# Two of six feed-forwards read their rows from a view 32 bytes in front of the first

## What is computed

```python
def swiglu(x, w_gu, w_down):
    g, u = jnp.split(x @ w_gu, 2, axis=-1)
    return (jax.nn.silu(g) * u) @ w_down
...
    y = modulate(rmsnorm(h, norm_ffn2[l]), sh3, sc3)
    h = h + 0.5 * gt3[:, None, :] * swiglu(y, w_ffn2_gu[l], w_ffn2_down[l])
```

## Time and profile before

| | |
|---|---|
| Three timed runs | 2493.82, 2497.54 and 2498.13 us, median 2497.54 us |
| Profiled execution, span | 2492.1 us, 39,334 instructions |
| TensorE busy | 2410.8 us (97%), 14,736 matmuls |
| VectorE, ScalarE, GpSimd busy | 1511.0, 892.0, 382.4 us |
| Mean granted TensorE clock | 0.985 |

### The profile page before, as it was taken

How to read it: one execution, slowest core, us unless ns; L and a number is a source line. 1 busy time by engine, 2 the same in 40 slices (tenths; PEclk the granted TensorE clock), 3 DMA queues, 4 the chain that set the end, 5 groups by cost and what they waited for, 6 DMA issues and landing times.

```text
span 2492.1 us, 39334 instructions
## 1 busy us (share of the span) xinstructions
PE 2410.8 (97%) x14736; PEld 2129.9 (85%) x14736; DVE 1511.0 (61%) x2434; ACT 892.0 (36%) x1103; POOL 382.4 (15%) x353
## 2 busy tenths in 40 slices
PE   6998989999999998999999999999999999999999
PEld 4998879999888888867778888888888889999999
DVE  7676768967878665355477786652222274555544
ACT  4443455454222223332232222242222242344443
POOL 2110531211111102332311111001110000000110
PEclk6999999999999999999999999999999999999999
DMA  7877746854655554211135555522222242135455
GB/s 280 284 263 274 259 141 222 275 196 159 218 185 194 180 168 150 81 64 51 68 115 202 185 179 190 172 85 101 101 80 90 99 149 81 68 104 184 169 186 168
DMA packets 79879, 400.19 MB, mean 161 GB/s; under 512 B 8817, under 2 KB 12913, under 8 KB 54705
## 3 DMA queue, kind: packets, MB, share of 16 engines
q1 hardware_dynamic: 77216, 393.39, 45.6%
q0 software_dynamic: 1056, 3.67, 0.5%
q10 hardware_dynamic: 1520, 1.95, 0.2%
HBM read 396.88 MB, written 2.10 MB: 160 GB/s over the span
## 4 chain that ended last, share of the span: by engine, by line
PE 46%; DVE 3%; ACT 1%; issue 0%; DMA 0%; ACTq 0%; DVEq 0%; SPq 0%
PE pg L1181 14%; PE pg L1182 13%; PE pg L1183 13%; PE pg L1359 1%; PE pg L1358 1%; PE pg L1360 1%; PE px L2003 1%; DVE wlo L2075 1%; PE px L1989 1%; DVE TMP L2244 0%; ACT whi L686 0%; PE px L1977 0%; DVE wlo L2080 0%; DMA raw<-w_d 0%; DVE Yl L2235 0%
## 5 line engine op out<-in xcount | busy, mean ns | idle before, releaser
L2080 DVE TENSOR_TENSOR wlo<-raw,whi 128x2048 fp32r<-128x2048 f32 (+1 forms) x202 | 415.6, 2057 | 504.0 <-ACT whi L691 503.5
L691 ACT ACTIVATE whi<-raw 128x2048 fp32r<-128x2048 f32 (+1 forms) x202 | 348.7, 1726 | 537.4 <-PE pg L1183 470.5
L1181 PE MATMUL pg<-Yh,whi 128*128 128x512 f32 (+1 forms) x1352 | 518.1, 383 | 11.6 <-DVE Yl L2303 2.6
L1182 PE MATMUL pg<-Yl,whi 128*128 128x512 f32 (+1 forms) x1352 | 513.0, 379 | 0.0
L1183 PE MATMUL pg<-Yh,wlo 128*128 128x512 f32 (+1 forms) x1352 | 512.8, 379 | 0.0
L1181 PE MATMUL pg<-YhB,whi 128*128 128x256 f32 (+1 forms) x1504 | 435.3, 289 | 20.5 <-DVE YlB L2235 7.6
L1182 PE MATMUL pg<-YlB,whi 128*128 128x256 f32 (+1 forms) x1504 | 428.4, 285 | 0.0
L1183 PE MATMUL pg<-YhB,wlo 128*128 128x256 f32 (+1 forms) x1504 | 428.2, 285 | 0.0
L1181 PEld LDWEIGHTS pg<-YhB,whi 128*128 128x128 f32 x1504 | 286.8, 191 | 31.2 <-issue 18.1
L1181 PEld LDWEIGHTS pg<-Yh,whi 128*128 128x128 f32 x1352 | 256.1, 189 | 67.2 <-issue 8.7
L1183 PEld LDWEIGHTS pg<-Yh,wlo 128*128 128x128 f32 x1352 | 256.1, 189 | 47.8
(11 more groups left out here) (378 smaller groups left out, 3642.1 us busy)
## 6 DMA issues: line engine op xcount, KB each, us to landing
raw<-w_t SPq DMA_DIRECT2D x194, 1024.0 KB, 5.1
ada<-w_ada SPq DMA_DIRECT2D x200, 512.0 KB, 3.6
raw<-w_d SPq DMA_DIRECT2D x96, 704.0 KB, 4.2
ADA<-w_ada SPq DMA_DIRECT2D x16, 512.0 KB, 13.9
NB<-na_bias POOLq DMA_DIRECT2D x8, 256.0 KB, 3.0
X<-x_t ACTq DMA_DIRECT2D x2, 512.0 KB, 15.8
spectrum<-HF POOLq DMA_DIRECT2D x1, 1024.0 KB, 10.3
X<-ctx_t SPq DMA_DIRECT2D x1, 1024.0 KB, 7.3
```

The source lines that it names most:

```text
L691: act.activation(whi[:, n % 2, 0:size], raw[:, n % 2, 0:size], ACT.Copy).then_inc(sem["hi_ready"], 1)
L1181: pe.matmul(out, w_hi, y_hi, start=first, stop=False)
L1182: pe.matmul(out, w_hi, y_lo, start=False, stop=False)
L2080: dve.tensor_tensor(wlo[:, n % 2, 0:size], raw[:, n % 2, 0:size], whi[:, n % 2, 0:size].bitcast(F32), ALU.subtract)\
```

## The change

A third view is added, 32 bytes in front of the first and so half-way between the two. The second feed-forward of layer 0 (`l0_gu2`, `l0_down2`, 512 tokens, first view before) and the second of layer 1, the last one (`l1_gu2`, `l1_down2`, 256 tokens, second view before) use it: their norms (`l0_2`, `l1_2`) write the normalised rows into it, their inner rows go into it, and their matmuls read from it. In `lead_pair`, which read `Hh` and `Hl` by name, the view is now asked for; for the two other down phases that end in it the answer is the same as before. No instruction is added, removed or moved on any engine: the two programs have the same 10,535 instructions in the same order, and differ in addresses.

```diff
-SHORT_ROWS = ("b1_0", "b1_gu1", "b1_1", "b1_in", "merge", "b1_out", "b1_2", "b1_gu2", "l1_1", "l1_in", "l1_2", "l1_gu2")
+MIDDLE_ROWS = ("l0_2", "l0_gu2", "l1_2", "l1_gu2")
+SHORT_ROWS = ("b1_0", "b1_gu1", "b1_1", "b1_in", "merge", "b1_out", "b1_2", "b1_gu2", "l1_1", "l1_in")
...
+    YhC = nc.alloc_sbuf_tensor_at("YhC", [P, 4096], F32R, offset=y_at - 32)
+    YlC = nc.alloc_sbuf_tensor_at("YlC", [P, 4096], F32R, offset=yl_at - 32)
...
+    HhC = nc.alloc_sbuf_tensor_at("HhC", [P, KF, 512], F32R, offset=region - 32)
+    HlC = nc.alloc_sbuf_tensor_at("HlC", [P, KF, 512], F32R, offset=hl_at - 32)
...
     def row_view(name):
 
+        if name in MIDDLE_ROWS:
+            return YhC8, YlC8
         return (YhB8, YlB8) if name in SHORT_ROWS else (Yh8, Yl8)
 
     def inner_of(name):
 
+        if name in ("l0_gu2", "l0_down2", "l1_gu2", "l1_down2"):
+            return HhC, HlC
         return (HhB, HlB) if INFO[name][2] == 256 else (Hh, Hl)
...
-                    return three(pg[1][:, stream, cols], whi[:, half, w], wlo[:, half, w], Hh[:, 11 * half + kt, cols], Hl[:, 11 * half + kt, cols],
+                    return three(pg[1][:, stream, cols], whi[:, half, w], wlo[:, half, w], inner_of(down)[0][:, 11 * half + kt, cols], inner_of(down)[1][:, 11 * half + kt, cols],
```

More of the change, by code:

```diff
@@ L309, in rhs_r @@
         return t[:, :].rearrange("p (c n) -> p c n", n=256)
-    Yh8, Yl8, YhB8, YlB8 = rhs_t(Yh), rhs_t(Yl), rhs_t(YhB), rhs_t(YlB)
+    Yh8, Yl8, YhB8, YlB8, YhC8, YlC8 = rhs_t(Yh), rhs_t(Yl), rhs_t(YhB), rhs_t(YlB), rhs_t(YhC), rhs_t(YlC)
     def row_view(name):
+        if name in MIDDLE_ROWS:
+            return YhC8, YlC8
         return (YhB8, YlB8) if name in SHORT_ROWS else (Yh8, Yl8)
     def inner_of(name):
+        if name in ("l0_gu2", "l0_down2", "l1_gu2", "l1_down2"):
+            return HhC, HlC
         return (HhB, HlB) if INFO[name][2] == 256 else (Hh, Hl)
```

## The result

Over six timed runs of each kernel the changed kernel took 2510.7 us in the median (2505.6 to 2518.3) and the kernel before 2495.7 (2489.3 to 2502.8). The ratio is **1.0064, 95% interval 1.0050 to 1.0078**: slower by 0.64%, about 16 us. The profiled execution after has a span of 2508.7 us, 16.6 us more than that of before.

What follows compares the result with a forecast made beforehand. TensorE was taken to bound the kernel, busy 97% of the span. Terms +5.2 + 5.2 - 0.4 = +10.0 us on 2497.5 gave 2507.5 us; forecast's own range 2502.5 to 2512.5, whole range 2493 to 2521 us.

Steps and rivals of the forecast that it cites:

- Direction and bound: In the four changed phases TensorE alone sets the time, so longer matmuls go into it one to one; slower 0.59.
- The term for 512 columns: l0_gu2 and l0_down2, first view to third: 1518 matmuls times 3.4 ns, +5.2 us, between 0 and +10.3.
- equally near both rows, so I take the mean: Third view lies 32 bytes from either known view, so 512 columns were priced at 230.1 ns, between 226.7 and 233.5.
- The term for 256 columns: l1_gu2 and l1_down2, second view to third: 1584 matmuls times 3.3 ns, +5.2 us, between 0 and +10.3.
- one width keeps its good pitch and the other takes the bad one: Second way to the middle of the sum: only one of 512 and 256 columns loses, +10.3 us either way.
- both widths in the bad state: Rival: third view as bad as the bad view for 512 and 256 columns, +20.6 us, 2518 us; chance 18%.
- The sign that it named: Pitch on YhC and HhC between 227 and 233 ns in l0_gu2 and l0_down2 in the profile after.
- No change: Rival: all pitches in the four phases stay, sum -0.9 to 0 us, 2497 us; chance 24%.
- The floor falls: Rival: third view escapes a sixteenth lost at both widths, gaining 30.9 us, 2466.6 us; gain over 5 us has 17%.
- The two pitches of the second view: 256 columns at 113.2 or 118.0 ns; in l1_in worth 2.8 us of either sign, left out of the sum.

## Why the prediction held, and where its sum was too small

**Direction and bound: right, and shown.** TensorE alone set the time of the four phases; 16.2 us more in them made 16.6 us more span, with no new wait and no other engine late. The order of instructions, the tail (2.80 us) and the norms stayed. Groups after, the norms' writes on the third view:

```profile
L743 ACT ACTIVATE YhC<-TMP,MOD 128x256 fp32r<-128x256 f32 x24 | 11.1, 503 | 9.3 <-DVE TMP L2253 9.3
L2244 DVE SCALAR_TENSOR_TENSOR YlC<-TMP,MOD,YhC 128x256 fp32r<-128x256 f32 x24 | 10.8, 480 | 0.8 <-ACT YhC L743 0.8
```

503 and 480 ns are the 501 to 506 and 480 of the earlier trace rows: these writes took the same time in all three views.

**The term for 512 columns: mis-sized by half.** It was 1518 times 3.4 ns, +5.2 us; it measured 1518 times 6.66, **+10.1**, its upper bound. The step that failed is "equally near both rows, so I take the mean". Nearness is no measure here: 16 bytes off the good place cost what 64 do.

**The term for 256 columns: mis-sized by a third.** It was +5.2 us and came to 1056 times 4.9 plus 528 times 4.7 ns, **+7.7** (6.6 in the two windows, which leave out a block and from which the wait in l1_down2 went). Here the mean was wrong for another reason: 113.2 and 119.7 are no ends of one scale, but one special place and an ordinary level of 117 to 120. lead_pair gained 0.2 us where 0.4 was forecast.

The sum by pitches is +17.6 us for the forecast's +10.0; the six runs of each say 16 (12 to 20). The reading "one width keeps its good pitch and the other takes the bad one", offered as a second way to the same sum, is false, since both lost. The nearest of the rivals was **both widths in the bad state**: at 512 exactly so, at 256 three quarters of the way.

That the time came out 3.2 us from the forecast (2510.7 for 2507.5) is partly luck. The forecast started from the median of three runs, 2497.5 us; over six runs the kernel before has 2495.7, so the medians differ by 15.0 us where 10.0 was forecast. That lies on the seam between the two cases that the prediction kept apart, its forecast (+5 to +15) and both widths bad (+15 to +23), and the pitches are nearer to the second. The sign that it named, 227 to 233 ns with 512 columns, was passed by 0.3.

**The other rivals.** *No change* is refuted by the pitches: a start moved by 16 bytes alone costs 6.7 ns at 512 columns. By the Trainium skill (SBUF — State Buffer, DMA port swizzle, the note on cachelines) an access that crosses into a new 16-byte line pays a penalty. By that alone no place tried here would differ, since all are whole lines; the traces, with 226.7 against 233.3 ns, show that it is not all that counts in a matmul's reads. *The floor falls* is refuted for the places tried: over eight starts for the rows, in steps of 16 bytes, and weights at three, no steady stretch at the full clock lay below 226.7 or 113.3 ns. The estimate from the Trainium skill (TensorE: Matmul & The Clock Gate, Back-to-back issue gap), 215.8 and 109.2 ns, showed in no run; the section calls its formula that of a matmul by itself. The two pitches of the second view, kept for the range at 2.8 us, are worth more than that: 4.6 us in l1_gu2 alone.

**Open.** What decides between 113.3 and 117.8 ns with rows at 64 is not settled: it changes between executions of unchanged phases, and within one. Why the distance between rows and weights counts for some pairs of starts and not for others isn't either, nor why place 112 had two pitches with 512 columns. The mechanism behind the places is therefore open; what is shown is which pairs of starts have which pitch. Why the good place of one width is the dearest of the other, and why even the good pitch stands a sixteenth above one column per cycle, is not settled either. For the long phases no place that was tried beats the ones of the kernel before. lead_pair and kind k of l1_in would each gain in another view, but they share their rows with matmuls of the other width; no faster version was run.

## What to carry to other kernels

Where TensorE is the bound, read its pitch by width and by the place where its rows and weights start, before touching either: with matmuls of 512 columns of 4-byte rows, start rows and weights at a multiple of 128 bytes, or expect some 3% in a phase that reads misplaced rows or weights throughout, and 2% where one tile of three is misplaced. With 256 columns, start the weights there and the rows 64 bytes off it; that pair, or the reverse, alone ever gave the good pitch, and not always. Price an unknown place by the ordinary level of places already seen, not by interpolating between them. And before a change of 0.2% is called a gain, look whether an unchanged phase has two pitches: here they are worth 4.6 us in one phase, 0.2% of the whole.

## What was not expected of the hardware

- The start of the loaded weights counts as much as that of the moving rows: 226.7 to 233.4 ns when only the weights moved by 64 bytes.
- One misplaced tile of three costs two thirds of the price (231.1 ns), part of it in a matmul whose own operands are well placed.
- One place gave two pitches in two kernels: 112 with 512 columns, 233.3 ns in l0_down1 and 236.6 in l0_down2.
- Rows and weights of 256 columns that all start at a multiple of 128 run at 119.8 ns, 5.7% above the 113.3 of rows at 64; with the weights moved by 64 and the rows left at 0, 113.3 was reached as well.
